# An HGRN head's inverse root: a power on GpSimd in place of a root on ScalarE and a reciprocal on VectorE

## The chip, the cores and the metric

One core of a Trainium2 chip. The metric is the device time of one execution of the whole program, in microseconds; three executions of the kernel before are known. The profile is of one further execution.

## The reference

One layer of a hybrid backbone on 640 tokens (512 latent, 128 context), model width 1024. Each layer normalizes, projects, runs two mixers side by side (a bidirectional HGRN2 recurrence with 4 heads of width 128, and a Hyena long convolution), projects back, and then runs a gated feed-forward part of width 2816. What matters here is how the HGRN heads' output is normalized:

```python
o = o_f + rev(o_b)                                            # (B, L, 4 heads, 128)
o = o * lax.rsqrt(jnp.mean(o * o, axis=-1, keepdims=True) + EPS)
o = o * p['hg_norm_w'][l].astype(F32).reshape(HG_HEADS, HG_DV)
o_hg = o.reshape(B, L, HG_WIDTH) * jax.nn.silu(g.astype(F32))
```

## The kernel before, in words

All products are made from two-part operands (a high part and the rest), three matmuls for one, so that TensorE has most of the work. Each engine has its own instruction list, written out by hand in a fixed order, and engines meet only at counting semaphores. `link` makes an engine wait for its own instruction.

The mixer's projections are made in 28 tiles of 128 output channels, each in two halves of 320 tokens: `n` counts the halves, 0 to 55. `half_product(n)` is 24 matmuls. Weights come by DMA on SP's queue into a ring `raw`; ScalarE copies each unit to `w_hi` (line 695), VectorE makes `w_lo` (line 1020), three tiles ahead of TensorE.

Between the halves each engine does one of the 12 steps of an HGRN head (`step_at(n)`): head h has its steps 0 to 11 at the halves 3 + 12h to 14 + 12h (those of the first head begin earlier). Step 0 is DIAG; steps 1 to 7 are levels of scores, where TensorE waits for VectorE's `qk_next` (QQ times gates, line 1221) and for ScalarE's `kc`; then KTURN, KV, OUT and, as step 11, NORM. OUT leaves the head's output in PSUM bank 6 (and 7), channels by tokens, and ScalarE squares it into `o_hg[:, h, :]`, 128x640. NORM on TensorE multiplies the squares with a matrix of ones (lines 1759 and 1760), so that the sum over the channels stands in every row of bank 4 (and 5). ScalarE makes the root of it (line 816), in `o_hg`, and raises `rms_ready`. VectorE's `finish_head(h)` waits for `rms_ready`, takes the reciprocal in place (line 1246), multiplies it with bank 6 and the norm's weight (line 1247) and with the gate `gs` (line 1249), and raises `heads_done`. Then VectorE goes on in its list: the diagonal's scores (line 1212), a width-3 convolution of a Hyena tile, KK, `w_lo`, QQ of the next head's level 0, and so on.

TensorE waits for `rms_ready` before DIAG of the next head (it writes bank 4), and for `heads_done` before step 1 of the next head (line 1731), which writes bank 6. Behind the fourth head the halves 51 to 55 have a `turn_u` each (line 1785); the one at half 53 waits for `heads_done` of all four.

GpSimd has one list as well. In the stage of the heads it holds only DMA issues: the masks and states, `gate_out(0)` (waits for a part of the modulation, `mod`), the store of each head's final state, the table `utab` into `tab`, `ptab`, and `gate_out(1)`. Its only arithmetic in the kernel is three additions of 128x512 at the start (line 645).

Of the kernel before, what the change touches and what calls it, by code (L numbers as in the profile page):

```python
# [21 lines left out]
ALU = mybir.AluOpType  # L22
ACT = mybir.ActivationFunctionType
AX = mybir.AxisListType

P = 128
# [3 lines left out]
T = TS + TP  # L30
# [8 lines left out]
HEADS = 4  # L39
# [268 lines left out]
def ap(t, offset, dims):  # L308

    base = t[:]  # L310
    return bass.AP(tensor=base.tensor, offset=offset, ap=[base.ap[0], *[list(d) for d in dims]])


def build(nc, io):
    ctx = ExitStack()

    def sb(stack, name, shape, dt=F32):
        return stack.enter_context(nc.sbuf_tensor(name, [P, *shape], dt))
# [3 lines left out]
    def sem(name):  # L322
        if name not in sems:
            sems[name] = ctx.enter_context(nc.semaphore(name))
        return sems[name]

    with ctx:
# [13 lines left out]
        ident = sb(ctx, "ident", [P])  # L341
        ones = sb(ctx, "ones", [P])
        eps = sb(ctx, "eps", [1])
        silu_c = sb(ctx, "silu_c", [KD, GROUP])
        mod = sb(ctx, "mod", [6 * KD, 2])
        gain = sb(ctx, "gain", [2, KD, 2])
# [39 lines left out]
        o_hg = sb(heads_v, "o_hg", [NC, T])  # L386
# [59 lines left out]
        def v(name, i=0, n=1):  # L446
            return vec[:, VEC[name] + i:VEC[name] + i + n]

        def banks(b, n=T, off=0):

            return ap(ps, b * 512 + off, [(1, n)])

        def linker(eng, own):


            count = {}

            def link(ins, name=None):
                name = name or own
                count[name] = count.get(name, 0) + 1  # L460
                ins.then_inc(sem(name), 1)
                eng.wait_ge(sem(name), count[name])
            return link
# [65 lines left out]
        def sizes(n):  # L529

            return ap((size, decay)[n % 2], 0, [(HW, 2), (1, HW)])
# [83 lines left out]
        @block.gpsimd  # L615
        def _(eng):
            def load(dst, src, name):
                eng.dma_start(dst, src).then_inc(sem(name), 16)

            def store_state(h):  # L620
                eng.wait_ge(sem("new_states"), h + 1)
                load(io["new_state"][0, 0].rearrange("d h k w -> h k d w")[h], newst[:, :, :], "state_stored")

            def gate_out(which):

                eng.wait_ge(sem("mod_ready"), ADA_ORDER.index(5 + 6 * which) + 1)
                col = (2 + 3 * which) * KD
                for s in range(2):
                    eng.dma_start(gates[which, s].rearrange("(k p) -> p k", p=P), mod[:, col:col + KD, s],
                                  allow_slow_non_contiguous=True).then_inc(sem("gate_out"), 16)  # L630

            load(vec[:, :], io["vec"], "ld_vec")
            for rows in (slice(0, NHID), slice(NHID, P)):
                load(w3[rows, :], io["hy_w3"][0], "ld_w3")
            load(decay[:, :, :], io["decay"], "ld_decay")
            load(ident[:, :], io["ident"], "ld_ident")
            load(ktab[:, :, :, :, :], io["ktab"], "ld_ktab")
            load(ptab_k[:, :, :], io["ptab"][:, 0], "ld_ktab")

            total = feats[:, 0:HW]  # L640
            for n in range(1, NT - 1):
                eng.wait_ge(sem("size_max"), n + 1)
                if n > 1:
                    eng.wait_ge(sem("size_added"), n - 1)
                nc.gpsimd.tensor_tensor(total, total, sizes(n)[:, 0, :], ALU.add).then_inc(sem("size_added"), 1)

            eng.wait_ge(sem("h_split"), KD)
            eng.wait_ge(sem("kspec_ready"), 5)
            load(ap(QQ, 0, [(P, LEVELS), (1, P)]).bitcast(U32), io["masks"], "ld_hg")
            load(state0[:, :, :, :], io["state_hgrn"][0, 0].rearrange("d h k w -> k d h w"), "ld_hg")  # L650
            gate_out(0)
            for h in range(HEADS - 1):
                store_state(h)

            eng.wait_ge(sem("head_steps"), (HEADS - 1) * STEPS + KTURN + 1)
            eng.wait_ge(sem("scores_taken"), HEADS * 8)
            load(tab[:, :].rearrange("p (a b c d) -> p a b c d", a=2, b=2, c=2), io["utab"], "ld_tab")
            store_state(HEADS - 1)

            eng.wait_ge(sem("head_steps"), HEADS * STEPS)  # L660
            load(ptab[:, :, :, :], io["ptab"][:, 1:3], "ld_ptab")
            gate_out(1)
            eng.wait_ge(sem("hy_conv"), 3 * NC)
            eng.wait_ge(sem("gate_out"), 4 * 16)
            load(grow1[:, :, :], gates[0].partition_broadcast(P), "ld_gate1")
            eng.wait_ge(sem("udft"), 4)
            load(tab[:, :].rearrange("p (a b c d) -> p a b c d", a=2, b=2, c=2), io["itab"], "ld_tab")


            for n in range(2):  # L670
                cols = slice(n * HW, (n + 1) * HW)
                eng.wait_ge(sem("raw_gated"), n + 1)
                eng.dma_start(x1[:, n, 0:NT - 1, :], io["x_sample"][0].rearrange("(i p) c -> p i c", p=P)[:, :, cols],
                              accum_op=ALU.add).then_inc(sem("ld_res"), 16)
                eng.dma_start(x1[:, n, NT - 1, :], io["x_prompt"][0][:, cols], accum_op=ALU.add).then_inc(sem("ld_res"), 16)
            eng.wait_ge(sem("zspec_ready"), 3)
            load(grow2[:, :, :], gates[1].partition_broadcast(P), "ld_gate2")
            load(fnw[:, :], io["final_norm_w"].partition_broadcast(P), "ld_fnw")
# [3 lines left out]
        def _(eng):  # L682
            link = linker(eng, "act_own")
            A = nc.scalar.activation
# [115 lines left out]
            def step(h, j):  # L800
                if j < KTURN - 1:
                    eng.wait_ge(sem("k_next"), 8 * h + j + 1)
                    if j:
                        eng.wait_ge(sem("head_steps"), h * STEPS + j)
                    A(kc[:, j % 2, :], ap(KK, 0, [(2 << j, T >> (j + 1)), (T + (1 << j), 2), (1, 1 << j)]),
                      ACT.Copy).then_inc(sem("kc_ready"), 1)
                if j == KTURN:
                    eng.wait_ge(sem("head_steps"), h * STEPS + KTURN + 1)
                    eng.wait_ge(sem("ada_cols"), ADA_EARLY + 2 * h + 1)
                    A(ktok[:, :, :, :], banks(4, 2 * 512), ACT.Copy).then_inc(sem("ktok_ready"), 1)  # L810
                if j == OUT:
                    eng.wait_ge(sem("head_steps"), h * STEPS + OUT + 1)
                    A(o_hg[:, h, :], banks(6), ACT.Square).then_inc(sem("osq_ready"), 1)
                if j == NORM:
                    eng.wait_ge(sem("head_steps"), h * STEPS + NORM + 1)
                    A(o_hg[:, h, :], banks(4), ACT.Sqrt, scale=1.0 / P, bias=eps[:, :]).then_inc(sem("rms_ready"), 1)

            def take_u(i):

# [15 lines left out]
            for n in range(NH):  # L835
# [35 lines left out]
                if step_at(n):  # L871
                    step(*step_at(n))
# [25 lines left out]
            for c in range(NC):  # L898
                eng.wait_ge(sem("z_made"), c + 1)
                if c:  # L900
# [3 lines left out]
                  scale=knorm[:, 1, c:c + 1]).then_inc(sem("z_taken"), 1)  # L904
                eng.wait_ge(sem("zp_made"), c + 1)
                A(zc[:, TS:T], ps[:, Z_BANKS[c % 2][1], 0:TP], ACT.Copy,
                  scale=knorm[:, 1, NC + c:NC + c + 1]).then_inc(sem("z_ready"), 1)
# [90 lines left out]
            for i in range(NT):  # L998
# [3 lines left out]
                  bias=stat[:, 0, 0, i:i + 1]).then_inc(sem("norm_ready"), 1)  # L1002
# [3 lines left out]
        def _(eng):  # L1006
            link = linker(eng, "dve_own")
            V = nc.vector
# [35 lines left out]

            V.memset(ones[:, :], 1.0).then_inc(sem("ones_ready"), 1)
            V.memset(silu_c[:, :, :], 0.0).then_inc(sem("ones_ready"), 1)
            V.memset(eps[:, :], EPS).then_inc(sem("ones_ready"), 1)
            eng.wait_ge(sem("ld_vec"), 16)
            lb = v("lb_f", 0, 2 * NC)
# [192 lines left out]

            def finish_head(h):

                eng.wait_ge(sem("rms_ready"), h + 1)
                link(V.reciprocal(o_hg[:, h, :], o_hg[:, h, :]))
                link(V.scalar_tensor_tensor(out=o_hg[:, h, :], in0=banks(6), scalar=v("hg_norm", h),
                                            in1=o_hg[:, h, :], op0=ALU.mult, op1=ALU.mult))
                link(V.tensor_tensor(o_hg[:, h, :], o_hg[:, h, :], gs[:, :], ALU.mult), "heads_done")

            def step(h, j):
                if j < KTURN:
                    take_level(h, j)
                elif j == KV:
                    make_states(h)
                elif j == NORM:
                    finish_head(h)
# [854 lines left out]
```

## Time and profile before

| | us |
|---|---|
| three executions | 971.9, 971.62, 965.82 |
| median | 971.62 |
| the profiled execution | 968.83 |
| its span, first to last instruction | 967.0 |

The profiled execution is 1.83 us longer than its span, and 2.8 us under the median. TensorE's granted clock was 0.989 of full over the span. Stretches are named by us from the span's start: the four heads' steps run from some 109 to 377 us, with NORM at 171, 238, 304 and 369 us.

### The profile page before, as it was taken

Reading aid. Unit: us, or ns where it says so; the run is one execution under the profiler, and the core shown is the slowest. Engines: PE = TensorE matmul, PEld = TensorE weight load, DVE = VectorE, ACT = ScalarE, POOL = GpSimd, SP = SyncE. Lnnn points to the kernel's source line nnn. Section 1 sums busy time; section 2 is a strip of 40 time slices with the busy share of each in tenths; the row PEclk is TensorE's granted clock in tenths of the full one; section 3 lists DMA queues with packets and bytes.
Section 4 is the critical chain, followed back from the end, with each engine's and each line's share of the span. In section 5 each row is a group of like instructions: output and inputs, shape, how many; then the busy total and the mean of one; then the engine's idle time right before and its main releaser. Section 6 shows DMA issues by size and latency. Waiting matters only on the chain.

```text
span 967.0 us, 13859 instructions
## 1 busy us (share of the span) xinstructions
PE 932.1 (96%) x5630; PEld 830.5 (86%) x5630; DVE 620.3 (64%) x809; ACT 339.3 (35%) x599; POOL 24.3 (3%) x34
## 2 busy tenths in 40 slices
PE   8988999999999999999999999999999999999996
PEld 4457889898898899687789899889999988999985
DVE  4844565884966976699586666445666644566655
ACT  2734243424333324233463433211333321233332
POOL 1100000100000000002000000000000000000000
PEclk9998999999999999999999999999999999999999
DMA  9746142343143334408121221222222221222102
GB/s 308 244 138 208 44 153 88 94 142 127 45 151 137 109 138 142 124 8 197 65 87 46 91 83 67 87 88 66 67 87 66 75 100 66 66 71 82 44 1 109
DMA packets 34407, 99.37 MB, mean 103 GB/s; under 512 B 3767, under 2 KB 11959, under 8 KB 33576
## 3 DMA queue, kind: packets, MB, share of 16 engines
q1 hardware_dynamic: 30760, 86.10, 26.8%
q0 software_dynamic: 3264, 12.35, 4.7%
q8 instruction: 45, 0.74, 0.3%
q14 instruction: 18, 0.15, 0.0%
q10 hardware_dynamic: 320, 0.04, 0.0%
HBM read 95.31 MB, written 3.16 MB: 102 GB/s over the span
## 4 chain that ended last, share of the span: by engine, by line
PE 79%; DVE 14%; ACT 3%; issue 2%; DMA 1%; ACTq 0%; DVEq 0%; SPq 0%
PE ps L1504 22%; PE ps L1505 22%; PE ps L1506 22%; PE ps L1731 3%; PE ps L1524 2%; DVE w_lo L1020 1%; PE ps L1743 1%; PE ps L1594 1%; PE ps L1868 1%; DMA hcol<-in_vec 1%; ACT w_hi L695 1%; PE ps L1751 1%; DMA raw<-in_slots 1%; PE ps L1532 0%; ACT xn L927 0%
## 5 line engine op out<-in xcount | busy, mean ns | idle before, releaser
L1504 PE MATMUL ps<-h_hi,w_hi 128*128 128x320 f32 x1152 | 362.6, 315 | 9.6 <-DVE w_lo L1020 5.4
L1505 PE MATMUL ps<-h_lo,w_hi 128*128 128x320 f32 x1152 | 357.6, 310 | 0.0
L1506 PE MATMUL ps<-h_hi,w_lo 128*128 128x320 f32 x1152 | 357.5, 310 | 0.0
L1504 PEld LDWEIGHTS ps<-h_hi,w_hi 128*128 128x128 f32 x1152 | 218.1, 189 | 11.2 <-ACT w_hi L695 4.4
L1505 PEld LDWEIGHTS ps<-h_lo,w_hi 128*128 128x128 f32 x1152 | 218.1, 189 | 0.1
L1506 PEld LDWEIGHTS ps<-h_hi,w_lo 128*128 128x128 f32 x1152 | 217.8, 189 | 0.0
L1020 DVE TENSOR_TENSOR w_lo<-raw,w_hi 128x1024 fp32r<-128x1024 f32 x106 | 129.4, 1225 | 112.7 <-ACT w_hi L695 109.1
L695 ACT ACTIVATE w_hi<-raw 128x1024 fp32r<-128x1024 f32 x106 | 110.8, 1052 | 94.1 <-PE ps L1506 91.6
L1505 PE MATMUL ps<-w_lo,a_hi 128*128 128x512 f32 x220 | 85.6, 389 | 0.0
L1504 PE MATMUL ps<-w_hi,a_hi 128*128 128x512 f32 x220 | 85.6, 389 | 0.0
L1506 PE MATMUL ps<-w_hi,a_lo 128*128 128x512 f32 x220 | 85.6, 389 | 0.0
L1039 DVE TENSOR_SCALAR cf<-padf,vec 128x648 f32<-128x648 f32 x44 | 24.5, 557 | 50.1 <-ACT padf L705 50.1
L1504 PE MATMUL ps<-w_hi,h_hi 128*128 128x512 f32 x120 | 50.5, 421 | 4.0 <-DVE knorm L1123 2.1
L1506 PEld LDWEIGHTS ps<-w_hi,a_lo 128*128 128x128 f32 x220 | 41.3, 188 | 8.6
L1504 PEld LDWEIGHTS ps<-w_hi,a_hi 128*128 128x128 f32 x220 | 41.3, 188 | 8.6
L1505 PEld LDWEIGHTS ps<-w_lo,a_hi 128*128 128x128 f32 x220 | 41.3, 188 | 8.4
L1506 PE MATMUL ps<-w_hi,h_lo 128*128 128x512 f32 x120 | 48.0, 400 | 0.0
L1505 PE MATMUL ps<-w_lo,h_hi 128*128 128x512 f32 x120 | 47.9, 399 | 0.0
L1731 PEld LDWEIGHTS ps<-QQ,kc 128*128 128x128 f32 x280 | 35.9, 191 | 10.5 <-issue 10.3
L985 ACT ACTIVATE a_hi<-actf 128x640 fp32r<-128x640 f32 x22 | 16.3, 740 | 79.7 <-DVE actf L1473 79.7
L1731 PE MATMUL ps<-QQ,kc 128*128 128x128 f32 x280 | 39.3, 288 | 2.9 <-issue 2.9
L1042 DVE SCALAR_TENSOR_TENSOR cf<-padf,vec,cf 128x648 f32<-128x648 f32 x44 | 39.3, 894 | 1.5
(267 smaller groups left out, 1041.3 us busy)
## 6 DMA issues: line engine op xcount, KB each, us to landing
raw<-in_slots SPq DMA_DIRECT2D x138, 512.0 KB, 3.7
raw<-in_slots SPq DMA_DIRECT2D x24, 256.0 KB, 6.7
xin<-in_x_sample SPq DMA_DIRECT2D x4, 512.0 KB, 10.4
grow<-gates POOLq DMA_DIRECT2D x2, 1024.0 KB, 13.2
x<-in_x_sample POOLq DMA_DIRECT2D x2, 1024.0 KB, 13.4
out_y_sample<-x SPq DMA_DIRECT2D x4, 512.0 KB, 3.1
decay<-in_decay POOLq DMA_DIRECT2D x1, 1280.0 KB, 10.4
ktab<-in_ktab POOLq DMA_DIRECT2D x1, 1024.0 KB, 12.3
```

The costliest lines, as they stand in the source:

```text
L695: A(w_hi[:, n % SPLITS, :], src, ACT.Copy).then_inc(sem("hi_ready"), 1)
L985: A(a_hi[:, f, :], actf[:, :], ACT.Copy).then_inc(sem("ahi_ready"), 1)
L1020: V.tensor_tensor(w_lo[:, n % SPLITS, :], raw[:, r % RING, :], w_hi[:, n % SPLITS, :].bitcast(F32), ALU.subtract).then_inc(sem("lo_ready"), 1)
L1039: link(V.tensor_scalar(out, pad[:, 1:1 + CONV], taps[1], None, ALU.mult))
L1042: link(V.scalar_tensor_tensor(out=out, in0=pad[:, 2:2 + CONV], scalar=taps[2], in1=out, op0=ALU.mult, op1=ALU.add), name)
L1504: mm(out, lhs[0], rhs[0], start=first, stop=False)
L1505: mm(out, lhs[0], rhs[1], start=False, stop=False)
L1506: return mm(out, lhs[1], rhs[0], start=False, stop=last)
L1524: last = mm(ps[g * GROUP:(g + 1) * GROUP, bank, :], silu_c[:, GROUPS * j + g, :], piece[:, g % 2 * HW:(g % 2 + 1) * HW], start=(j == 0), s ...
L1594: last = mm(ps[:, 4 + 2 * cs + e, :], ktab[:, cs, e, k, m * P:(m + 1) * P], filt[:, cs, 2 * e + k, :], start=(k == 0), stop=(k == 1))
L1731: last = mm(chunk(h, j, c), kc[:, l % 2, c * P:(c + 1) * P], ap(QQ, c * P, [(2 * s, P // (2 * s)), (T + s, 2), (1, s)]), start=True, stop= ...
L1743: last = mm(ps[:, 4 + d, n * P:(n + 1) * P], ktok[:, d, n, :], vtok[:, c, h * P:(h + 1) * P], start=True, stop=True)
```

## The change

ScalarE's pass at NORM becomes an Identity with the same scale and bias, so that `o_hg` holds the mean square plus EPS. GpSimd then raises this tile of 128x640 to the power -0.5 in place, with an exponent read from a new one-column tile `power`, and raises a new semaphore `rms_made`. VectorE waits for that one and has no reciprocal any more. In GpSimd's list, the power of head h stands right behind the store of head h's state, and `gate_out(0)`, until now ahead of all the stores, is put behind the power of head 0. The power of head 3 is ahead of the issue of `ptab` and of `gate_out(1)`.

```diff
+        power = sb(ctx, "power", [1])
...
-            gate_out(0)
+            def rms(h):
+                eng.wait_ge(sem("rms_ready"), h + 1)
+                nc.gpsimd.tensor_tensor(o_hg[:, h, :], o_hg[:, h, :], ap(power, 0, [(0, T)]), ALU.pow).then_inc(sem("rms_made"), 1)
+
             for h in range(HEADS - 1):
                 store_state(h)
+                rms(h)
+                if h == 0:
+                    gate_out(0)
...
             store_state(HEADS - 1)
 
+            rms(HEADS - 1)
             eng.wait_ge(sem("head_steps"), HEADS * STEPS)
             load(ptab[:, :, :, :], io["ptab"][:, 1:3], "ld_ptab")
             gate_out(1)
...
-                    A(o_hg[:, h, :], banks(4), ACT.Sqrt, scale=1.0 / P, bias=eps[:, :]).then_inc(sem("rms_ready"), 1)
+                    A(o_hg[:, h, :], banks(4), ACT.Identity, scale=1.0 / P, bias=eps[:, :]).then_inc(sem("rms_ready"), 1)
...
+            V.memset(power[:, :], -0.5)
             V.memset(eps[:, :], EPS).then_inc(sem("ones_ready"), 1)
...
-                eng.wait_ge(sem("rms_ready"), h + 1)
-                link(V.reciprocal(o_hg[:, h, :], o_hg[:, h, :]))
+                eng.wait_ge(sem("rms_made"), h + 1)
                 link(V.scalar_tensor_tensor(out=o_hg[:, h, :], in0=banks(6), scalar=v("hg_norm", h),
```

## Rows read from the trace of the kernel before

**Rows 1.** The page: engine totals, and shares of the chain that ended last

```profile
PE 932.1 (96%) x5630; PEld 830.5 (86%) x5630; DVE 620.3 (64%) x809; ACT 339.3 (35%) x599; POOL 24.3 (3%) x34
...
PE 79%; DVE 14%; ACT 3%; issue 2%; DMA 1%; ACTq 0%; DVEq 0%; SPq 0%
```

**Rows 2.** Timeline, VectorE, after head 0's norm: start, us, line, idle before

```profile
173.68 4.15 DVE L1246 RECIPROCAL o_hg<-o_hg 128x640 f32<-128x640 f32 x1 [3.65 <-ACT o_hg L816]
177.87 0.88 DVE L1247 SCALAR_TENSOR_TENSOR o_hg<-ps,vec,o_hg 128x640 f32<-128x640 f32 x1
178.79 0.83 DVE L1249 TENSOR_TENSOR o_hg<-o_hg,gs 128x640 f32<-128x640 f32 x1
...
185.98 1.40 DVE L1221 TENSOR_TENSOR QQ<-QQ,TT 128x640 f32<-128x640 f32 x1
```

**Rows 3.** Timeline, ScalarE, the same stretch

```profile
171.03 1.28 ACT L816 ACT_TABLE_LOAD   x1
172.85 0.80 ACT L816 ACTIVATE o_hg<-ps,eps 128x640 f32<-128x640 f32 x1 [0.53 <-PE ps L1760]
```

**Rows 4.** Timeline, TensorE, the same stretch and on to 206 us

```profile
172.43 0.38 PE L1760 MATMUL ps<-o_hg,ones 128*128 128x128 f32 x2
...
181.23 1.82 PE L1731 MATMUL ps<-QQ,kc 128*128 128x128 f32 x10
...
187.48 1.44 PE L1731 MATMUL ps<-QQ,kc 128*128 128x128 f32 x10 [0.90 <-issue]
...
204.73 0.66 PE L1532 MATMUL ps<-ident,ktok 128*128 128x128 f32 x4 [0.64 <-ACT ktok L712]
```

**Rows 5.** Timeline, TensorE, the same place after heads 1 and 2

```profile
254.28 1.44 PE L1731 MATMUL ps<-QQ,kc 128*128 128x128 f32 x10 [1.11 <-issue]
...
320.03 1.44 PE L1731 MATMUL ps<-QQ,kc 128*128 128x128 f32 x10 [0.91 <-issue]
```

**Rows 6.** Groups of instructions by line: count, busy us, mean ns, idle before

```profile
L1246 DVE RECIPROCAL o_hg<-o_hg 128x640 f32<-128x640 f32 x4 | 16.6, 4152 | 14.6 <-ACT o_hg L816 14.6
...
L816 ACT ACT_TABLE_LOAD x4 | 5.1, 1283 | 0.1
```

**Rows 7.** Line 645, GpSimd's only arithmetic: ns min/median/max, first and last start

```profile
L645 POOL TENSOR_TENSOR feats<-feats,decay x2: 1266/1279/1292, 43.2 to 48.8; 128x512 f32<-128x512 f32 x2
L645 POOL TENSOR_TENSOR feats<-feats,size x1: 1802/1802/1802, 46.9 to 46.9; 128x512 f32<-128x512 f32 x1
```

**Rows 8.** Timeline, VectorE: a pass over as many elements as line 645's

```profile
46.12 0.69 DVE L1110 TENSOR_TENSOR size<-size 128x512 f32<-128x512 f32 x1
46.85 0.69 DVE L1110 TENSOR_TENSOR decay<-decay 128x512 f32<-128x512 f32 x1
```

**Rows 9.** Timeline, TensorE after head 3: product and turn ahead of the wait

```profile
382.57 0.63 PE L1785 MATMUL ps<-ident,u_hy 128*128 128x128 f32 x4
```

**Rows 10.** Timeline, VectorE after head 3

```profile
376.78 0.83 DVE L1249 TENSOR_TENSOR o_hg<-o_hg,gs 128x640 f32<-128x640 f32 x1
```

**Rows 11.** Timeline, TensorE: the one long stall early on

```profile
80.16 0.61 PE L1504 MATMUL ps<-h_hi,w_hi 128*128 128x320 f32 x1 [4.05 <-DVE w_lo L1020]
```

**Rows 12.** Stretches around that stall: us, busy per engine, PEclk, DMA

```profile
76.10:80.16 4.06, 0.01 (x2) 0.03 (x1) 3.92 (x6) 4.06 (x6) 1.06 (x2) 0.82 0.24 96
80.16:85.36 5.20, 5.20 (x19) 5.20 (x20) 1.03 (x1) 1.88 (x2) 0.41 (x1) 0.50 0.95 302
```

**Rows 13.** Timeline, GpSimd's queue around the heads

```profile
186.24 1.78 POOL L629 DMA_DIRECT2D gates<-mod  x2 [105.67 <-DVE mod L1080]
...
352.40 0.59 POOL L618 DMA_DIRECT2D tab<-in_utab  x1 [56.66 <-PE ps L1738]
...
371.10 0.58 POOL L618 DMA_DIRECT2D ptab<-in_ptab  x1 [9.92 <-PE ps L1760]
```

**Rows 14.** Timeline, ScalarE: the next root behind the heads

```profile
460.32 0.29 ACT L912 ACTIVATE sq<-x 128x128 f32<-128x128 f32 x1
465.55 0.30 ACT L914 ACTIVATE rhy<-rhy,eps 128x5 f32<-128x5 f32 x1 [4.94 <-DVE rhy L1383]
```

## The prediction

> **What bounds the kernel.** The page comes first: TensorE is busy 96% of the span, VectorE 64%, GpSimd 3%, and the chain that ended last lies 79% on TensorE and 14% on VectorE [rows 1]. So the price of an edit on VectorE, ScalarE or GpSimd is what it moves of TensorE's waits. The change touches four places, one behind each head. I read these in the timelines of VectorE, ScalarE and TensorE, looking for the wait of TensorE that ends last behind `finish_head`.
>
> Behind head 0, ScalarE's root ends at 173.65 and VectorE, which has sat idle for it, runs the reciprocal in 4.15 us, then two passes; `heads_done` is up at 178.79 + 0.83 = 179.62 [rows 2, 3]. TensorE needs it for step 1 of the next head, which it starts at 181.23 [rows 4]: a margin of 1.6 us. But VectorE goes on without a gap to QQ, done at 185.98 + 1.40 = 187.38 [rows 2], and TensorE, idle for 0.90 us, starts step 2 at 187.48, right behind it [rows 4]. So at step 2 there is no margin at all; VectorE's list is late there. The same wait stands behind head 1 with 1.11 and behind head 2 with 0.91 us [rows 5]. After head 0 there is one more, of 0.64 us at 204.73 [rows 4], at the end of a stretch in which VectorE, late by its list, freed the weight ring late. Behind head 3 it is another matter: `heads_done` is up at 376.78 + 0.83 = 377.61 [rows 10], and TensorE comes to the wait for it at 382.55 [rows 9]: a margin of 4.9 us.
>
> **The change, part by part.** Call X the time of one power on GpSimd, and D the delay of `heads_done`. Before, 4.22 us pass from the root's end to the start of the pass on line 1247 (173.65 to 177.87) [rows 2, 3]. After, they are X and two hand-overs. GpSimd's addition at 46.9 began 0.09 us behind the VectorE pass that it waited for (46.12 + 0.69), and VectorE takes 0.03 us behind ScalarE [rows 2, 3, 7, 8]. So D = X + 0.12 - 4.22 = X - 4.1.
>
> *What D costs.* Behind heads 0, 1 and 2, a positive D goes to step 2 in full, since VectorE's list has no gap in between: D each. Behind head 3, D less 4.9. If D is negative, the gain ends with TensorE's own idle time: 0.90 + 0.64 + 1.11 + 0.91 = 3.6 us in all [rows 4, 5].
>
> *The reciprocal removed.* Four of 4.15 us [rows 6], already in D.
>
> *ScalarE's root to Identity.* The pass has the same shape and operands as before: I take its 0.80 us [rows 3] as unchanged. Four loads of a function table go, 1.28 us each [rows 6]. The load ran from 171.03 to 172.31, ScalarE then sat idle 0.53 us, and the root began at 172.85, 0.04 us behind the matmul of line 1760 (172.43 + 0.38) [rows 3, 4]. The load was hidden in ScalarE's wait: I take nothing for it. What hides it is that the root is always issued ahead of NORM's end. The table is needed again later: the next root (line 914) now needs a load of its own, and ScalarE is idle 4.94 us before it [rows 14], so that is hidden too. The Trainium skill speaks against "nothing": ScalarE: Activation LUTs, What ACT_TABLE_LOAD costs, gives 1.28 us and a drain of 1.38 us behind it, 2.66 us in all. By that the root would have begun at 173.69, and the change would get back 0.84 us a head; the row has the 1.28 us, but the root at 172.85, so this trace shows no such delay.
>
> *The power itself.* No row has one. GpSimd's additions of 128x512 took 1.27 to 1.29 us undisturbed, and 1.80 us where a VectorE pass over two tiles of SBUF ran beside it [rows 7, 8]. For 640 columns that is 1.28 x 1.25 = 1.60 us a pass. VectorE is waiting for this very result, so nothing disturbs it. The lower bound is one pass, 1.6 us. For more: on VectorE a reciprocal over 128x640 costs 4.15 us and a plain pass 0.83 [rows 2], so 5 passes for one such function. A power is a logarithm, a product and an exponential. At 5 passes for each function that is 11 passes, 17.6 us: my value, an estimate and the weakest number here; I take it over the 5 passes (8.0 us) of a single function because two functions are chained. If each of the two needs double (more terms, special cases) it is 22 passes, 35.2 us: the upper end that I carry. With X = 17.6, D = 13.5: three times 13.5 is 40.5, and behind head 3 it is 13.5 - 4.9 = 8.6.
>
> *TensorE's clock.* The one long stall in the trace is 4.05 us, ended by `w_lo` [rows 11]; the granted clock over it is 0.82, and over the next 5.20 us it is 0.50, the level of 1.2 GHz in place of 2.4, with TensorE busy throughout [rows 12]. That lost 2.6 us. A D of 13.5 stalls TensorE for 11.9 us at step 1, so this comes behind each head. Behind heads 0 to 2 it costs nothing, though: from `heads_done` to QQ's end VectorE takes 7.76 us, TensorE from step 1 to its wait at step 2 only 5.35 (181.23 to 187.48 - 0.90) [rows 2, 4], and the 2.6 us fall in that gap. Behind head 3 there is no such gap: 2.6 us.
>
> *GpSimd's queue.* `gate_out(0)` was issued at 186.24 and would have held up head 0's power there; moved behind it, it is late by X at most, and its reader comes behind `gate_out(1)`, some 200 us on. The stores of the states go out as early or earlier. `utab`, issued at 352.40 once its semaphores are up, is behind head 2's power (from 307 us on): late only if X is over 45 us. `ptab`, issued at 371.10, goes behind head 3's power; its reader comes after the turns that are delayed too. All at nothing [rows 13]. The added memset is one column at the start: nothing.
>
> **Sum.** 40.5 + 8.6 + 2.6 = 51.7 us. On the profiled execution's 968.8 that is 1020.5; on the median of the runs, 971.6, it is 1023, which I give. Since the clock term is paid once, 35.2 us (D = 31.1) gives 93.3 + 26.2 + 2.6 = 122, 1094.
>
> **The rivals.** First, the other side: *the power is nearly a plain pass*, X under 4.1. The point that decides is 4.1 us. TensorE loses its waits at step 2, 3.6 us in all: 968. For it speaks that a GpSimd pass is cheap beside VectorE's slow reciprocal; against it, that VectorE itself needs 5 passes for one such function. Chance 0.12.
>
> Second, *one function's worth*: X of 4.1 to 12, with 5 passes of GpSimd as its middle, 8.0 us. D = 3.9, three times, nothing behind head 3: 11.7 us, 983. Within 1% it stays up to X = 7.3 (3 x 3.2 = 9.6). Chance 0.26, of which 0.12 is within 1%. The Trainium skill's rule on such work (GPSIMD Engine Reference, Engine selection) is that GpSimd is about 2 times slower than VectorE with two inputs; the trace agrees for an addition, 1.28 to 0.69 us [rows 7, 8]. Held against the reciprocal's 4.15 us it would make X 8.3 us, and the result this rival's.
>
> Third, *two functions at double cost*, X of 25 to 45: 1094 at 35. Chance 0.20. Fourth, *the power is worked out element by element, not a column at once*: at 60 passes, 96 us, D = 92, 276 + 87 + 2.6 = 366, 1337, and `utab` late on top. Nothing in the trace excludes it. Chance 0.10.
>
> **How the numbers follow.** My forecast, X of 12 to 25, has 0.32. The range from 967 to 1094 takes in the first and second rival, the forecast and half of the third, and leaves out the fourth and half of the third, 0.20. About 1% is what a measurement of this kernel can tell from no change. Faster by more than that can't come out of 3.6 us, except by scatter: 0.02. Within 1%: 0.12 + 0.12 less that, 0.22. Slower: 0.76.
>
> **What the profile after would show.** A row of GpSimd, 128x640, four times: its mean is X. VectorE's idle time ahead of line 1247 in the place of the reciprocal, 3.7 us and then X more. TensorE's waits behind heads 0 to 2: one at step 1 of D - 1.6, one at step 2 that shrinks or goes under the slow clock; behind head 3 one at half 53 of D - 4.9. No table load on ScalarE in the heads, one near 461 us. The prediction is wrong if X is far from 17.6 us; if X is right and the time is not, then the delay was not handed on in full three times, or the clock took longer to come back.

## The result, and the profile after

| | us |
|---|---|
| the changed kernel, median of 4 runs | 1360.89 (1359.82 to 1361.37) |
| the kernel before beside it, median of 4 | 970.19 |
| ratio, 95% interval | 1.4048 [1.4007, 1.4089] |

The change costs 390.7 us. The page of the changed kernel: span; busy time of each engine; TensorE's busy tenths and granted clock in 40 slices; the chain by engine; and two groups of instructions (busy us, mean ns, idle before).

```profile
span 1358.7 us, 13857 instructions
...
PE 942.2 (69%) x5630; PEld 836.5 (62%) x5630; DVE 603.4 (44%) x806; ACT 335.4 (25%) x596; POOL 433.8 (32%) x38
...
PE   8889930089100990019900399999999999999997
...
PEclk9999975589655995559955699999999999999999
...
PE 53%; POOL 30%; DVE 11%; ACT 2%; issue 1%; DMA 1%; ACTq 0%; DVEq 0%; SPq 0%
...
L656 POOL TENSOR_TENSOR o_hg<-o_hg,power 128x640 f32<-128x640 f32 x4 | 409.4, 102361 | 42.1 <-ACT o_hg L826 42.1
...
L1257 DVE SCALAR_TENSOR_TENSOR o_hg<-ps,vec,o_hg 128x640 f32<-128x640 f32 x4 | 3.5, 884 | 424.4 <-POOL o_hg L656 424.4
```

GpSimd's power over 128x640 takes 102.36 us, four times. It is 30% of the chain that ended last; in [rows 1] GpSimd wasn't in it. TensorE is busy for 942 us as against 932: it does the same work and waits, in four blocks of slices at 0 to 3 tenths, in and behind which the clock's row stands at 5 to 7 tenths. The largest waits (in total, times, longest):

```profile
DVE o_hg L1257 <- POOL o_hg L656: 424.4, 4, 106.1
...
PE ps L1741 <- DVE o_hg L1259: 289.8, 3, 96.6
...
PE ps L1795 <- DVE o_hg L1259: 93.2, 1, 93.2
```

VectorE waits 106.1 us for each power, where it waited 3.65 for the root [rows 2]. TensorE stands at step 1 for `heads_done` three times and once at the turn of half 53. Its timeline behind head 0, the places of [rows 4]:

```profile
276.83 2.47 PE L1741 MATMUL ps<-QQ,kc 128*128 128x128 f32 x10 [96.62 <-DVE o_hg L1259]
...
284.56 1.44 PE L1741 MATMUL ps<-QQ,kc 128*128 128x128 f32 x10 [0.27 <-issue]
```

96.62 us of idle time at step 1, then 0.27 at step 2, where there were none and 0.90. Stretches of the same kernel, with busy time of PE, PEld, DVE, ACT and POOL, then the granted clock:

```profile
181.00:276.80 95.80, 0.00 (x0) 0.00 (x1) 1.79 (x3) 0.00 (x0) 93.90 (x1) 0.51 0.00 0
276.80:282.00 5.20, 5.17 (x21) 5.20 (x22) 5.03 (x6) 0.52 (x1) 0.00 (x0) 0.50 0.01 3
282.00:284.60 2.60, 2.33 (x15) 2.10 (x14) 2.50 (x5) 0.60 (x3) 1.30 (x2) 0.92 0.33 82
769.20:775.00 5.80, 5.72 (x26) 5.73 (x27) 5.52 (x10) 1.55 (x2) 1.47 (x2) 0.59 0.24 75
```

In the stall the clock is at 0.51, for the first 5.2 us of work at 0.50 (1.2 GHz in place of 2.4), and then it comes back: a mean of 0.92 over the next 2.6 us is some 0.4 us more at the lower level and the rest at the upper. Behind head 3 it is 0.59 over 5.8 us, which is some 4.8 us at the lower level. The wait there, as [rows 9]:

```profile
769.28 1.13 PE L1795 MATMUL ps<-ident,u_hy 128*128 128x128 f32 x4 [93.17 <-DVE o_hg L1259]
...
779.84 5.75 PE L1878 MATMUL ps<-ut,tab 128*128 128x512 f32 x13
```

On ScalarE the table load ahead of line 826 (line 816 before) is gone. The pass over 128x640 has kept its 0.80 us, and the idle time before it has grown to 1.83 us, close to the 0.53 of [rows 3] and the load's 1.28 together:

```profile
171.65 0.80 ACT L826 ACTIVATE o_hg<-ps,eps 128x640 f32<-128x640 f32 x1 [1.83 <-PE ps L1770]
```

The load now stands ahead of the next root, and ScalarE still waits for VectorE after it, as [rows 14] had room for:

```profile
850.28 1.28 ACT L924 ACT_TABLE_LOAD   x1
852.87 0.30 ACT L924 ACTIVATE rhy<-rhy,eps 128x5 f32<-128x5 f32 x1 [1.30 <-DVE rhy L1393]
```

### The profile page after: what moved, and what is told of

Read it like the earlier page. It is cut to its first block, busy times and chain, and to the rows that moved or that the text cites. A ratio compares the mean times of both kernels' runs of the same rounds, so it can differ in the third digit from the quotient of the medians.

```text
span 1358.7 us, 13857 instructions
## 1 busy us (share of the span) xinstructions
PE 942.2 (69%) x5630; PEld 836.5 (62%) x5630; DVE 603.4 (44%) x806; ACT 335.4 (25%) x596; POOL 433.8 (32%) x38
## 4 chain that ended last, share of the span: by engine, by line
PE 53%; POOL 30%; DVE 11%; ACT 2%; issue 1%; DMA 1%; ACTq 0%; DVEq 0%; SPq 0%
POOL o_hg L656 30%; PE ps L1514 15%; PE ps L1515 15%; PE ps L1516 15%; PE ps L1741 2%; PE ps L1534 1%; DVE w_lo L1030 1%; DMA raw<-in_slots 1%; DMA w<-in_hy_w 1%; PE ps L1753 1%; PE ps L1604 1%; PE ps L1878 1%; DVE KK L1217 0%; ACT w_hi L705 0%; PE ps L1761 0%
## 5 line engine op out<-in xcount | busy, mean ns | idle before, releaser
L656 POOL TENSOR_TENSOR o_hg<-o_hg,power 128x640 f32<-128x640 f32 x4 | 409.4, 102361 | 42.1 <-ACT o_hg L826 42.1
L1257 DVE SCALAR_TENSOR_TENSOR o_hg<-ps,vec,o_hg 128x640 f32<-128x640 f32 x4 | 3.5, 884 | 424.4 <-POOL o_hg L656 424.4
L815 ACT ACTIVATE kc<-KK 128x640 f32<-128x640 f32 x28 | 22.2, 793 | 339.3 <-DVE KK L1217 332.0
L1795 PE MATMUL ps<-ident,u_hy 128*128 128x128 f32 x20 | 3.6, 310 | 93.2 <-DVE o_hg L1259 93.2
L1795 PEld LDWEIGHTS ps<-ident,u_hy 128*128 128x128 f32 x20 | 2.9, 193 | 93.4 <-DVE o_hg L1259 93.4
L619 POOL DMA_DIRECT2D out_new_state<-newst x4 | 2.9, 723 | 179.7 <-DVE newst L1252 179.7
```

Source lines behind the costliest of these rows:

```text
L656: nc.gpsimd.tensor_tensor(o_hg[:, h, :], o_hg[:, h, :], ap(power, 0, [(0, T)]), ALU.pow).then_inc(sem("rms_made"), 1)
```

## The experiments

Fourteen kernels ran. Where the text says "of the changed kernel", that is its base, otherwise the kernel before.

### Is it the power, or the way over GpSimd?

**e1_plain_pass**, of the changed kernel:

```diff
-... ap(power, 0, [(0, T)]), ALU.pow).then_inc(sem("rms_made"), 1)
+... ap(power, 0, [(0, T)]), ALU.mult).then_inc(sem("rms_made"), 1)
```

Expected: 

> The changed kernel with GpSimd's power replaced by a multiplication over the same 128x640 tile, so the root is left out (the mean square is only scaled). All waits and the order of GpSimd's list stay. Theory: the whole loss is the length X of GpSimd's pass, handed on as D = X - 4.1 behind each head. A plain pass is 1.6 us, D = -2.5, TensorE loses its waits at step 2: 967 us (3.6 under the kernel before). Rival: the hand-over over GpSimd itself, the changed order of its list or a load of code costs a part of the 391 us: then this kernel is clearly above 971.

Measured: 968.51 us to 968.56 for the kernel before, ratio 0.9999 [0.9983, 1.0016]. GpSimd's pass (its timeline) takes 1.25 us:

```profile
174.22 1.25 POOL L656 TENSOR_TENSOR o_hg<-o_hg,power 128x640 f32<-128x640 f32 x1 [10.54 <-ACT o_hg L826]
```

So the hand-over over GpSimd and the new order of its list cost nothing that shows, and the 391 us come from the power (all but some 4 of them, as e11 will show). But the 3.6 us of gain that I expected didn't come either. The trace has them: from the squares of head 0 to those of head 3 (first to last start) it took 193.4 us in place of 198.0, and TensorE's waits at step 2 are gone. They were lost again where the change does nothing: from the start of VectorE's last cast of the feed-forward input (`h_hi<-hf`, line 1034, now 1044) to the end it took 464.3 us in place of 460.1. That led to e5 and e6.

### What sets the power's time?

**e2_power_64**, of the changed kernel:

```diff
-nc.gpsimd.tensor_tensor(o_hg[:, h, :], ..., ap(power, 0, [(0, T)]), ALU.pow).then_inc(...)
+nc.gpsimd.tensor_tensor(o_hg[:, h, P // 2:T], ..., ap(power, 0, [(0, T - P // 2)]), ALU.mult)
+nc.gpsimd.tensor_tensor(o_hg[:, h, 0:P // 2], ..., ap(power, 0, [(0, P // 2)]), ALU.pow).then_inc(...)
```

Expected: 

> The changed kernel, with the power over 64 of the 640 columns and a multiplication over the other 576 (their root is left out). If the power costs a fixed 102.36 / 640 = 0.160 us a column, it takes 10.2 us and the multiplication 1.4, X = 11.7, D = 7.6: three times 7.6 plus 2.7 behind head 3 is 25.5, some 996 us, with the clock's fall hidden behind heads 0 to 2. Rival: a large fixed part for each call (starting or fetching the power's code), say half of the 102 us: then the power takes over 50 us and the kernel some 1170.

Measured: 997.16 us, ratio 1.0298 [1.0270, 1.0325]. GpSimd's timeline, and TensorE's at steps 1 and 2:

```profile
173.93 1.14 POOL L656 TENSOR_TENSOR o_hg<-o_hg,power 128x576 f32<-128x576 f32 x1 [10.52 <-ACT o_hg L827]
175.03 10.55 POOL L657 TENSOR_TENSOR o_hg<-o_hg,power 128x64 f32<-128x64 f32 x1
```

```profile
187.51 2.47 PE L1742 MATMUL ps<-QQ,kc 128*128 128x128 f32 x10 [5.90 <-DVE o_hg L1260]
...
195.21 1.44 PE L1742 MATMUL ps<-QQ,kc 128*128 128x128 f32 x10 [1.02 <-issue]
```

From 64 to 640 columns the power goes from 10.55 to 102.36 us. If it grows evenly between these two sizes, the only ones that were run, it is 0.159 us a column (91.81 / 576), and 0.35 us that doesn't depend on the columns. There is no large fixed part. The two passes take 11.65 us together, from 173.93 to 185.58, so D = 11.65 + 0.12 - 4.22 = 7.55; TensorE waits 5.90 at step 1 (D less its margin of 1.6) and 1.02 at step 2. The sum of the terms is 3 x 7.55 + 2.65 = 25.3; measured are 28.6 (997.16 - 968.56), and the missing 3.3 us are of the size that e5 finds, below.

**e3_power_one_row**, of the changed kernel:

```diff
-nc.gpsimd.tensor_tensor(o_hg[:, h, :], o_hg[:, h, :], ap(power, 0, [(0, T)]), ALU.pow)
+nc.gpsimd.tensor_tensor(o_hg[0:1, h, :], o_hg[0:1, h, :], ap(power, 0, [(0, T)])[0:1], ALU.pow)
```

Expected: 

> The changed kernel, with the power over one row (partition 0) of 640 columns in place of 128 rows (the root is left out in the other rows). Theory A, all rows of a column are worked at once, 0.160 us a column: X stays 102 us and the kernel near 1361. Theory B, the rows that one GpSimd core holds are worked one after another: X falls to the time of one row, a sixteenth if a core has 16 rows, 6.4 us, D = 2.3, the kernel some 979.

**e4_exponent_one**, of the changed kernel: `V.memset(power[:, :], 1.0)` in place of -0.5.

Expected: 

> The changed kernel with the exponent 1 in place of -0.5 (so the root is left out). If the power takes the same way whatever its operands, X stays 102.4 us and the kernel 1361. Rival: the time depends on the values (a short cut for simple exponents, a reciprocal behind negative ones): X is then another, and the kernel's time moves by 4 times the difference.

Measured, one run each: 1359.69 and 1360.58 us. The power of head 0, of e3 and of e4:

```profile
171.75 102.37 POOL L656 TENSOR_TENSOR o_hg<-o_hg,power 1x640 f32<-1x640 f32 x1 [10.53 <-ACT o_hg L826]
```

```profile
172.61 102.37 POOL L656 TENSOR_TENSOR o_hg<-o_hg,power 128x640 f32<-128x640 f32 x1 [10.54 <-ACT o_hg L826]
```

It takes 102.37 us in both. Fewer rows save nothing, nor does a simple exponent. The price is one of columns; leaving out rows is no way to lower it. Whether GpSimd works the rows of a column at once, or one after another whether they are asked for or not, one row can't tell; theory B as stated has fallen. Whether the time depends on the numbers that are raised to the power, or on their type, was not tried.

### Where did the gain of the plain pass go?

The diff of **e5_tile_only** is one line, behind `eps`; nothing reads the tile:

```diff
         eps = sb(ctx, "eps", [1])
+        power = sb(ctx, "power", [1])
```

Expected: 

> The kernel before with one edit: the unused one-column tile named power behind eps. It takes 32 bytes of each partition, so each tile behind it, a_hi and a_lo among them, lies 32 bytes further on. Theory: this shift is what took back the gain of the plain pass: in its trace the heads were 4.1 us shorter than before, and the feed-forward stage, which the change doesn't touch, 4.2 us longer, with the matmuls that read a_hi at 396 ns where the kernel before had 389. Then this kernel shows 396 ns too and is some 4 us slower than the kernel before (ratio 1.004). Rival: the matmuls differ from one execution to the next, and the profile of before fell on a quick one: ratio 1.000.

**e6_plain_pass_no_shift** is e1 with the exponent in a second column of `eps`:

```diff
-        power = sb(ctx, "power", [1])
+        pair = sb(ctx, "eps", [2])
+        eps = pair[:, 0:1]
```

Expected: 

> The plain pass on GpSimd again (the root is left out), with the exponent in a second column of the tile eps, so that no tile lies elsewhere than in the kernel before. If the shift is what took back the gain, the heads' gain shows now: 4 us under the kernel before, ratio 0.996. Rival, that the gain is lost behind the heads in any case (another wait) or that executions differ by chance: ratio 1.000.

Measured: e5 971.35 us, ratio 1.0041 [1.0027, 1.0055]; e6 963.59 us, ratio 0.9961 [0.9948, 0.9974]. The kernel before had a median of 968.71 us beside them; by the medians alone e5 loses 2.6 us and e6 gains 5.1, by the ratios it is 4.0 and 3.8. One group of the feed-forward products in both (the 220 matmuls of one of the three lines that read `a_hi`: busy us, mean ns), first e5, then e6:

```profile
L1506 PE MATMUL ps<-w_lo,a_hi 128*128 128x512 f32 x220 | 87.0, 396 | 0.0
```

```profile
L1515 PE MATMUL ps<-w_lo,a_hi 128*128 128x512 f32 x220 | 85.6, 389 | 0.0
```

The shift theory holds. With the tile the group has 396 ns, and without it 389, as in the kernel before, whose group is this:

```profile
L1505 PE MATMUL ps<-w_lo,a_hi 128*128 128x512 f32 x220 | 85.6, 389 | 0.0
```

Three lines with 220 matmuls each and 6 to 7 ns more for each matmul make some 4.3 us. The tile moves everything behind it by 32 bytes in each partition. The changed kernel has the same 396 ns:

```profile
L1515 PE MATMUL ps<-w_lo,a_hi 128*128 128x512 f32 x220 | 87.0, 396 | 0.0
```

**e11_power_no_shift** is the changed kernel with the exponent placed as in e6.

Expected: 

> The changed kernel as it is, but with the exponent in a second column of the tile eps, so that no tile lies elsewhere than before. If the two causes add up, it is 4 us below the changed kernel, some 1357, and what is left, 388 us over the kernel before, is the power alone. Rival: behind the long stalls the shift costs nothing more: 1361.

Measured: 1356.69 us, ratio 1.4008 [1.3990, 1.4026]: 4.2 us below the changed kernel. This kernel is 388.0 us over the kernel before beside it (968.65), and no tile lies elsewhere in it. So the result is some 388 us of the power and some 3 to 4 us of the tile's place.

Which place counts? Five more runs have the kernel before with an unused tile of another size or place:

```diff
+        power = sb(ctx, "power", [16])     e9_tile_64_bytes, behind eps
+        power = sb(ctx, "power", [32])     e12_tile_128_bytes, behind eps
+        sb(late, "power", [1])             e10_only_late_shifted, ahead of a_hi
+        sb(late, "power", [128])           e13_late_512_bytes, ahead of a_hi
+        sb(late, "power", [1024])          e14_late_4096_bytes, ahead of a_hi
```

(e10 is the one with the size of e5.) Expected of e9: 

> The kernel before with an unused tile of 16 columns behind eps: it takes 64 bytes, so a_hi and a_lo lie 64 bytes further on and begin at a multiple of 64 again. If it is the start within 64 bytes that counts, the matmuls that read them are back at 389 ns and the kernel is as before, ratio 1.000. Rival: any shift costs (another tile's place, or what lies beside what): 396 ns and 1.004, as with 32 bytes.

Expected of e10: 

> The kernel before with an unused one-column tile at the start of the late group, so that only a_hi, a_lo, padf, cf, actf and tmpd lie 32 bytes further on, and nothing of the mixer. If the 4 us come from the feed-forward products' operands alone: 396 ns, ratio 1.004. Rival: they come from the tiles of the first part of the kernel: 389 ns or a ratio of 1.000.

Expected of e12: 

> The kernel before with an unused tile of 32 columns behind eps, so that all tiles behind it lie 128 bytes further on. a_hi lies at 155,776 bytes in the kernel before, a multiple of 128, and was slow at 32 and at 64 bytes more. If a start at a multiple of 128 bytes is what counts, the matmuls that read a_hi and a_lo are at 389 ns again and the ratio is 1.000. Rival: the place itself counts (a distance to another tile, a bank), or any new tile does: 396 ns and 1.004.

Expected of e13: 

> The kernel before with an unused tile of 128 columns at the start of the late group: a_hi and a_lo lie 512 bytes further on. If a coarser start than 128 bytes counts (256 or 512), 389 ns and a ratio of 1.000. If the distance to the weights' tiles modulo 4096 counts, or any shift: 396 ns and 1.004 to 1.006.

Expected of e14: 

> The same with 1024 columns: a_hi and a_lo lie 4096 bytes further on, so that their distance to w_hi, w_lo and raw is a multiple of 4096 bytes again. If that distance counts: 389 ns and a ratio of 1.000. If any shift costs: 396 ns and 1.004 to 1.006.

| run | a_hi moved by, bytes | ns of those matmuls | ratio, 95% interval |
|---|---|---|---|
| e5 | 32 | 395 to 396 | 1.0041 [1.0027, 1.0055] |
| e10, late group alone | 32 | 395 to 396 | 1.0059 [1.0045, 1.0073] |
| e9 | 64 | 395 to 396 | 1.0037 [1.0024, 1.0049] |
| e12 | 128 | 395 | 1.0037 [1.0021, 1.0053] |
| e13, late group alone | 512 | 389 | 1.0003 [0.9984, 1.0022] |
| e14, late group alone | 4096 | 389 | 1.0000 [0.9983, 1.0018] |

The group of e12, then that of e13:

```profile
L1506 PE MATMUL ps<-w_lo,a_hi 128*128 128x512 f32 x220 | 86.8, 395 | 0.0
```

```profile
L1506 PE MATMUL ps<-w_lo,a_hi 128*128 128x512 f32 x220 | 85.6, 389 | 0.0
```

My guess of a start at a multiple of 64, then of 128 bytes, fell both times. A shift by 512 or 4096 bytes is free, one by 32, 64 or 128 is not; 256 was not tried. A rounder start alone doesn't help: in e12 `a_hi` begins at 155,776 + 128 = 155,904 bytes, a multiple of 256, and is slow, and in the kernel before its start is no multiple of 256, and it is fast. What the three fast places share is the distance to `w_hi`: it was 118,784 bytes, a multiple of 512, and it still is one after a shift by 512 or 4096. They share the remainder of the start by 512 as well, so whether the start itself or this distance counts stays open. e10 shows that the late group alone is enough for the loss. That it lost more than e5 is not clear of the noise: the two intervals overlap, and from the start of VectorE's last `h_lo<-hf,h_hi` (the other half of the feed-forward input's split) to the end e10's profiled execution took 462.2 us and e5's 463.7.

### The table loads

**e7_identity_only**: in the kernel before, `ACT.Sqrt` becomes `ACT.Identity`; the reciprocal stays.

Expected: 

> The kernel before with Identity in place of the root on ScalarE, the reciprocal kept (the root is left out). It prices the four table loads alone. My theory: they were hidden, the kernel is as before, ratio 1.000. Rival, the page's drain behind each load: 0.84 us for each of three heads, 2.5 us less, ratio 0.997.

Measured: 967.79 us, ratio 0.9997 [0.9979, 1.0015]. ScalarE at head 0's norm has no load, and waits 1.84 us instead:

```profile
171.81 0.80 ACT L816 ACTIVATE o_hg<-ps,eps 128x640 f32<-128x640 f32 x1 [1.84 <-PE ps L1760]
```

The loads were worth nothing that shows: the interval leaves room for 2 us at most.

### A version that beats both

**e8_log_exp**:

```diff
-A(o_hg[:, h, :], banks(4), ACT.Sqrt, scale=1.0 / P, bias=eps[:, :]).then_inc(sem("rms_ready"), 1)
+link(A(o_hg[:, h, :], banks(4), ACT.Ln, scale=1.0 / P, bias=eps[:, :]))
+A(o_hg[:, h, :], o_hg[:, h, :], ACT.Exp, scale=-0.5).then_inc(sem("rms_ready"), 1)
...
-link(V.reciprocal(o_hg[:, h, :], o_hg[:, h, :]))
```

Expected: 

> The kernel before with the inverse root as a logarithm and an exponential on ScalarE (scale 1/128 and bias EPS into the first, scale -0.5 into the second), and no reciprocal on VectorE; no new tile. ScalarE's pass is now two of 0.8 us with a wait between, and the reciprocal's 4.15 us are gone: D = 0.9 - 4.15 = -3.3, past TensorE's own idle time, so the heads give back some 4 us: 965, ratio 0.996. Rival: logarithm and exponential lie in different table sets, and a second load of 1.28 us goes on the path in each head: D is still negative, -2, and the gain about the same for heads 0 to 2; if the loads hold up ScalarE's copies of weights or kc, the gain is gone.

Measured: 962.58 us, ratio 0.9951 [0.9939, 0.9963], 0.5% below the kernel before. ScalarE at head 0, and VectorE's pass behind it:

```profile
170.22 1.28 ACT L816 ACT_TABLE_LOAD   x1
172.04 0.80 ACT L816 ACTIVATE o_hg<-ps,eps 128x640 f32<-128x640 f32 x1 [0.54 <-PE ps L1760]
172.86 1.28 ACT L817 ACT_TABLE_LOAD   x1
174.15 0.74 ACT L817 ACTIVATE o_hg<-o_hg 128x640 f32<-128x640 f32 x1
```

```profile
174.92 0.88 DVE L1247 SCALAR_TENSOR_TENSOR o_hg<-ps,vec,o_hg 128x640 f32<-128x640 f32 x1 [5.71 <-ACT o_hg L817]
```

The rival was right about the loads: a second one stands on the path, 1.28 us between the two passes. The exponential ends 2.05 us after the logarithm; the reciprocal and its start took 4.22. So D = 174.92 - 172.84 - 4.22 = -2.14, and TensorE has no wait left at steps 1 and 2 of the next heads. From the squares of head 0 to those of head 3 it takes 193.9 us in place of 198.0. This is what the change was after, with two passes of 0.8 us on ScalarE in place of one of 102 on GpSimd.

## Why the prediction was wrong

- **What bounds the kernel, and who is handed D: right.** From the root of head 0 to that of head 3 the changed kernel takes 492.5 us (171.7 to 664.2), the kernel before 197.9 (172.9 to 370.8): 294.6 more. With X = 102.36, D is 98.3, and three times D is 294.8. From head 3's root to the first matmul of line 1868 (1878 now) it is 115.6 in place of 20.2, 95.4 more; the terms say 93.4 and 2.6 for the clock, 96.0.
- **TensorE's clock: right.** By the stretches above, the lower level held for some 5.6 us of work behind head 0 and some 4.8 behind head 3, against some 5.4 in the trace of the kernel before (5.2 in [rows 12], and the next 0.5 us had 0.83), although the stalls were about 24 times as long as the one there. Behind head 0 TensorE's wait at step 2 shrank from 0.90 to 0.27 us (behind heads 1 and 2 it is 0.73 and 0.68), so that the slow clock fell in VectorE's gap, and behind head 3 it cost. By the prediction's own numbers that gap was 7.76 - 5.35 = 2.4 us, a little under the 2.6 that were said to fall in it; the wait that was left shows that they did.
- **The power itself: wrong, and this is the step that failed.** "At 5 passes for each function that is 11 passes, 17.6 us" - measured were 102.36 us, 82 of GpSimd's plain passes over the same tile (1.25 us in e1). With the measured X the sum is 294.8 + 93.4 + 2.6 = 390.8; with mine it was 51.7. That 390.8 meets the measured 390.7 is in part luck: the measured time holds some 4 us of the tile's place, which the sum has not, and e11, without them, is 388.0, 2.8 under the sum. In the profiles the three delays are all there; most of what is missing lies behind head 3, where from its squares to the last `h_lo<-hf,h_hi` e11 took 94.0 us more than the kernel before, against 96.0. In the profiles of kernels that don't change this stretch it differs by up to 3 us (141.1 in e5, 144.3 in e10). The 5 passes were VectorE's price for a reciprocal. Nothing in the trace said that GpSimd pays for a function in the same ratio to its own addition as VectorE does, and I stretched this to 22 passes for the upper end and no further. The second rival took the Trainium skill's factor of 2 for elementwise work with two inputs (GPSIMD Engine Reference, Engine selection): against VectorE's reciprocal of 4.15 us the factor for the power is 25. The fourth rival, 60 passes and 1337 us, was the nearest, at 0.10. Its 60 passes had been worked out from no row, so that it came near is luck, and its reason (element by element, and not a column at once) is not shown: one row takes as long as 128. The range left it out by design. With no row for this operation on this engine, the upper bound was open, and the range should have said so.
- **The plain pass in 1.6 us: too long.** The multiplication over 640 columns took 1.25 us, no more than the additions of 512 [rows 7]; its second operand is one column read again and again, theirs were two full tiles. No decision hung on it.
- **The gain that a short X would bring: right in kind.** e6 gains 0.39%, 3.8 us by its ratio; 3.6 was the sum of TensorE's waits. From the squares of head 0 to those of head 3 it takes 193.2 us in place of 198.0, so 4.8 less, somewhat more than these waits.
- **The reciprocal and the table loads: right.** e7 finds nothing for the loads. The Trainium skill, ScalarE: Activation LUTs, What ACT_TABLE_LOAD costs, speaks of a drain of 1.38 us beside each load; in [rows 3] and in e7 no such delay shows. In e8 the next activation began 0.01 us after a load had ended.
- **A term that I didn't have:** the one-column tile, "nothing" in the prediction, costs some 4 us by moving other tiles. It is 1% of the result, but as much as the whole gain that the change could have brought.
- **GpSimd's queue: right in its price, even at 102 us.** e1 has the changed order and loses nothing by it. The prediction held `utab` to be late with X over 45 us, and the fourth rival put that on top of its sum. It was not late: head 2's power ended at 603.55, and GpSimd then waited 42.22 us more for TensorE, which the same delays had moved back.

```profile
645.76 0.60 POOL L619 DMA_DIRECT2D tab<-in_utab  x1 [42.22 <-PE ps L1748]
```

## What to carry to other kernels

Before a function is moved to an engine that has never run it in this kernel, time one such instruction by itself: this kernel's power on GpSimd cost 0.16 us for each column, with one row as with 128. A step between two engines that has a margin of 1.6 us on one side and none on the other hands on nearly all of its delay, once for each time around the loop. And when a change adds a tile, put it where it moves nothing, or compare the time of untouched matmuls before and after.

## What was not expected of the hardware

- GpSimd's power, float32, takes 0.159 us a column and 0.35 us beside that (from 64 and 640 columns), the same for 1 and for 128 rows and for the exponents -0.5 and 1; a multiplication takes 1.25 us for 640 columns.
- Matmuls with 512 moving columns whose other operand is `a_hi` or `a_lo` took 389 ns in the kernel before, and 395 to 396 when these tiles began 32, 64 or 128 bytes further on; at 512 and 4096 bytes it was 389 again.
- After stalls of 96.62 and 93.17 us TensorE's granted clock was at 0.50 for some 5.6 and 4.8 us of work, and after a stall of 4.05 us for some 5.4: the way back took about as long after a stall 24 times as long.
